# The matrix memories' query convolution moved from VectorE to TensorE as diagonal products

## What is computed

```python
def short_conv(a, w, b, n_ctx):
    a_ctx, a_lat = a[:, :n_ctx], a[:, n_ctx:]
    lat = lax.conv_general_dilated(a_lat.reshape(bsz, rows, GRID_W, ch), w[:, :, None, :], (1, 1), 'SAME', ...)
    ctx = lax.conv_general_dilated(a_ctx, w[CONV_K // 2][:, None, :], (1,), 'SAME', ...)
    return jnp.concatenate([ctx, lat.reshape(bsz, s_lat, ch)], axis=1) + b
...
qk = jax.nn.silu(short_conv(jnp.concatenate([ml_q, ml_k], axis=-1), conv_w, conv_b, n_ctx))
mq, mk = jnp.split(qk, 2, axis=-1)
```

## Time and profile before

| | |
|---|---|
| median of 3 runs | 3661.3 us (3655.49 to 3663.13) |
| the profiled execution | 3671.62 us, span 3668.6 us |
| busy over the span | PE 3333.2 us, DVE 1671.9 us, ACT 1162.1 us, POOL 975.9 us |
| busy from 2215 to 2269 us (54 us) | PE 15.41, DVE 50.84, ACT 21.05, POOL 2.35 us |

### The profile page before, as it was taken

The page is one execution under the profiler, slowest core; times in us unless marked ns, Lnnn a source line. Parts: engine busy times, 40 slices in busy tenths (PEclk is TensorE's granted clock), DMA queues, the critical chain, the costliest instruction groups (busy, mean ns, idle before and its releaser), DMA issues. The chain is left out here.

```text
span 3668.6 us, 42188 instructions
## 1 busy us (share of the span) xinstructions
PE 3333.2 (91%) x17058; PEld 2636.7 (72%) x17058; DVE 1671.9 (46%) x2620; ACT 1162.1 (32%) x1873; POOL 975.9 (27%) x418
## 2 busy tenths in 40 slices
PE   4999989989999799999998875989999888889998
PEld 3887767867888588888787662368887664568887
DVE  5995566554331323355500997532211585631211
ACT  2232364224443322122332213333223224533222
POOL 0001322433444122322332110024443220024443
PEclk7999999998999799999999997889999888889999
DMA  4232324441223122334321000012232110013332
GB/s 178 92 98 91 130 95 154 154 166 64 98 95 95 61 86 93 126 133 139 112 75 58 18 18 6 1 62 95 97 110 88 52 46 26 1 58 98 96 94 86
DMA packets 91197, 315.98 MB, mean 86 GB/s; under 512 B 10742, under 2 KB 12534, under 8 KB 90234
## 3 DMA queue, kind: packets, MB, share of 16 engines
q1 hardware_dynamic: 88060, 303.69, 25.6%
q10 hardware_dynamic: 2944, 9.60, 0.7%
HBM read 311.16 MB, written 2.10 MB: 85 GB/s over the span
## 5 line engine op out<-in xcount | busy, mean ns | idle before, releaser
L245 POOL TENSOR_TENSOR terms<-streams,terms 128x1024 fp32r<-128x1024 f32 (+2 forms) x414 | 975.6, 2357 | 2670.8 <-ACT terms L233 2670.8
L454 PE MATMUL bank<-terms,terms 128*128 128x512 f32 (+2 forms) x3936 | 1477.4, 375 | 49.1 <-DVE terms L721 17.7
L455 PE MATMUL bank<-terms,terms 128*128 128x512 f32 (+2 forms) x3936 | 1468.9, 373 | 0.0
L456 PE MATMUL bank<-terms,terms 128*128 128x512 f32 (+2 forms) x3936 | 1467.1, 373 | 0.0
L233 ACT ACTIVATE terms<-streams 128x1024 fp32r<-128x1024 f32 (+1 forms) x462 | 475.5, 1030 | 1802.1 <-PE bank L456 1624.8
L454 PEld LDWEIGHTS bank<-terms,terms 128*128 128x128 f32 x3936 | 749.3, 190 | 200.8 <-issue 52.1
L456 PEld LDWEIGHTS bank<-terms,terms 128*128 128x128 f32 x3936 | 749.1, 190 | 129.2
L455 PEld LDWEIGHTS bank<-terms,terms 128*128 128x128 f32 x3936 | 750.9, 191 | 123.5
L1642 DVE TENSOR_TENSOR stage<-stage,bank 128x256 f32<-128x256 f32 (+1 forms) x88 | 54.6, 621 | 596.6 <-ACT stage L1632 596.6
L1085 DVE SCALAR_TENSOR_TENSOR arena<-arena,vec 128x512 f32<-128x512 f32 x240 | 162.5, 746 | 0.2
L1625 DVE TENSOR_TENSOR terms<-stage,terms 128x512 fp32r<-128x512 f32 (+1 forms) x66 | 116.5, 1769 | 0.0
(11 more groups left out here) (334 smaller groups left out, 3133.1 us busy)
## 6 DMA issues: line engine op xcount, KB each, us to landing
streams<-in_ffn_w SPq DMA_DIRECT2D x104, 512.0 KB, 3.5
streams<-in_w_mod SPq DMA_DIRECT2D x72, 512.0 KB, 3.5
streams<-in_w_up SPq DMA_DIRECT2D x44, 512.0 KB, 3.5
streams<-in_w_gu SPq DMA_DIRECT2D x44, 512.0 KB, 3.5
streams<-in_w_ada SPq DMA_DIRECT2D x32, 512.0 KB, 3.5
streams<-in_w_down SPq DMA_DIRECT2D x32, 512.0 KB, 3.6
streams<-in_w_v SPq DMA_DIRECT2D x24, 512.0 KB, 3.8
streams<-in_ffn_w SPq DMA_DIRECT2D x24, 384.0 KB, 3.3
```

The lines of the kernel that those rows point to most:

```text
L245: gp.tensor_tensor(self.low(m), self.raw(n), self.high(m), ALU.subtract).then_inc(self.low_made.sem, 1)
L454: pe.matmul(out, high[:, at], x_high, start=kk == start, stop=False)
L455: pe.matmul(out, high[:, at], x_low, start=False, stop=False)
L456: mm = pe.matmul(out, low[:, at], x_high, start=False, stop=kk == kts - 1)
```

## The change

The two query tiles are no longer convolved by taps. ACT makes 18 weight matrices of 128x128 out of the identity, one for each tile and tap: the identity scaled by that tap's weight of each channel, a diagonal matrix. PE multiplies each with the shifted grid and accumulates the nine taps of a tile in one PSUM bank, in plain float32. ACT then adds the bias and takes the SiLU straight from the bank. DVE keeps the 24 taps of the keys, in the order 0 to 9, reciprocals, 9 to 15, scaling, 15 to 24.

```diff
+ML_DIAG = B2_QG + 1536
...
+    def diagonals(self, act):
+        for t in range(2):
+            for tap in range(9):
+                ins = act.activation(self.diagonal(t, tap), k.ident[:, :], ACT.Copy, scale=k.v("mconv_w", 9 * t + tap))
+            ins.then_inc(self.weights_made.sem, 1)
+
+    def smoothed(self, pe, t):
+        bank, uses = self.banks[t]
+        if uses:
+            pe.wait_ge(self.k.bank_free[bank].sem, uses)
+        pe.wait_ge(*self.weights_made(t + 1))
+        for tap in MIDDLE_FIRST:
+            r, c, rx, cx = self.ranges(tap)
+            mm = pe.matmul(grid(self.k.bank[bank][:, :])[:, r, c], self.diagonal(t, tap), grid(self.plain(t))[:, rx, cx],
+                           start=tap == 4, stop=tap == 8)
+        mm.then_inc(self.queries_in.sem, 1)
+
+    def queries_kept(self, act, t):
+        act.wait_ge(*self.queries_in(t + 1))
+        act.activation(self.queries[t], self.k.bank[bank][:, :], ACT.Silu, bias=self.k.v("mconv_b", t)
+                       ).then_inc(self.k.bank_free[bank].sem, 1)
...
-                            inputs.tapped: 42})
+                            inputs.tapped: 24, inputs.weights_made: 2, inputs.queries_in: 2})
+        inputs.banks = [k.take_bank() for _ in range(2)]
...
         self.heads.widened(pe)
+        for t in range(2):
+            self.inputs.smoothed(pe, t)
 
     def scalar(self, act):
         self.heads.squares(act)
+        act.wait_ge(*self.k.dve_done(HEADS2))
+        self.inputs.diagonals(act)
         self.heads.roots(act)
         self.gates.scalar(act)
         self.chain.softplus(act, self.gates)
-        act.wait_ge(*self.inputs.tapped(42))
         for t in range(2):
-            act.activation(self.inputs.queries[t], self.inputs.queries[t], ACT.Silu)
+            self.inputs.queries_kept(act, t)
+        act.wait_ge(*self.inputs.tapped(24))
+        for t in range(2):
             act.activation(self.inputs.keys[:, t, :], self.inputs.keys[:, t, :], ACT.Silu)
 
     def vector(self, dve):
...
-        self.inputs.taps(dve, 0, 12)
+        self.inputs.taps(dve, 0, 9)
         self.heads.inverses(dve)
-        self.inputs.taps(dve, 12, 24)
+        self.inputs.taps(dve, 9, 15)
         self.heads.scaling(dve)
-        self.inputs.taps(dve, 24, 42)
+        self.inputs.taps(dve, 15, 24)
```

More of the change, by code:

```diff
@@ L2050, in __init__ @@
         self.k = k
-        self.tapped = k.more[12]
+        self.tapped, self.weights_made, self.queries_in = k.more[12:15]
         k.bank_set, k.bank_turn = [3], 0
@@ L2104, in there, with ranges @@
         for t in range(2):
-            self.of_queries.evicted(eng, t)
             for c in range(2):
                 self.of_keys.evicted(eng, t, c)
+    def ranges(self, tap):
+        dy, dx = tap // 3 - 1, tap % 3 - 1
+        r, c = slice(max(0, -dy), 8 - max(0, dy)), slice(max(0, -dx), 64 - max(0, dx))
+        return r, c, slice(r.start + dy, r.stop + dy), slice(c.start + dx, c.stop + dx)
     def taps(self, eng, a, b):
@@ L2115, in tap @@
         k = self.k
-        t, j = divmod(n, 9) if n < 18 else (2 + (n - 18) // 12, (n - 18) % 12)
+        t, j = divmod(n, 12)
         if n:
@@ L2119, in tap @@
         if j < 9:
[L2120 to L2126, removed]
+            tap = MIDDLE_FIRST[j]
+            r, c, rx, cx = self.ranges(tap)
+            y, x = grid(self.keys[:, t, CTX:])[:, r, c], grid(self.plain(2 + t))[:, rx, cx]
+            w, first = k.v("mconv_w", 9 * (2 + t) + tap), j == 0
         else:
@@ L2130, in tap @@
             c = slice(max(0, -dx), CTX - max(0, dx))
-            y, x = self.keys[:, t - 2, c], self.context(t - 2)[:, c.start + dx:c.stop + dx]
-            w, first = k.v("mconv_w", 9 * t + 3 + tap), j == 9
+            y, x = self.keys[:, t, c], self.context(t)[:, c.start + dx:c.stop + dx]
+            w, first = k.v("mconv_w", 9 * (2 + t) + 3 + tap), j == 9
         if first:
-            ins = eng.tensor_scalar(y, x, w, k.v("mconv_b", t), ALU.mult, ALU.add)
+            ins = eng.tensor_scalar(y, x, w, k.v("mconv_b", 2 + t), ALU.mult, ALU.add)
         else:
@@ L2137, in tap, with diagonal @@
         ins.then_inc(self.tapped.sem, 1)
+    def diagonal(self, t, tap):
+        at = ML_DIAG + P * (9 * t + tap)
+        return self.k.arena[:, at:at + P]
+    def diagonals(self, act):
+        k = self.k
+        for t in range(2):
[8 more added lines that the diff above has]
+        for tap in MIDDLE_FIRST:
+            r, c, rx, cx = self.ranges(tap)
+            mm = pe.matmul(grid(self.k.bank[bank][:, :])[:, r, c], self.diagonal(t, tap), grid(self.plain(t))[:, rx, cx],
+                           start=tap == 4, stop=tap == 8)
+        mm.then_inc(self.queries_in.sem, 1)
+    def queries_kept(self, act, t):
+        bank, _ = self.banks[t]
+        act.wait_ge(*self.queries_in(t + 1))
+        act.activation(self.queries[t], self.k.bank[bank][:, :], ACT.Silu, bias=self.k.v("mconv_b", t)
+                       ).then_inc(self.k.bank_free[bank].sem, 1)
+MIDDLE_FIRST = (4, 0, 1, 2, 3, 5, 6, 7, 8)
 class MemoryStart(Pass):
```

## The result

In the first measurement the changed kernel takes 3642.56 us (median of 5, 3640.98 to 3644.66) against 3661.3 (5 runs, 3655.49 to 3666.45): the ratio is 0.9947, 95% interval 0.9936 to 0.9958, a gain of 19 us where 11.6 were forecast. Four more comparisons in three later sessions gave 8.0, 15.4, 9.9 and 12.8 us. (The ratio is not the quotient of the medians, which lie 9.3, 17.7, 9.7 and 10.2 us apart there; a gain worked out from a ratio is that share of the median of the kernel before.) The block itself is 10.8 to 10.9 us shorter in every trace.

What follows compares the result with a forecast made beforehand. DVE was taken to bound the query convolution's block; taking 11.6 us off it brings the profiled execution from 3671.6 to 3660.0, and 10.3 less for the median gives 3649.7 us. Its own range was 3645 to 3654, the whole range 3642 to 3657.

Steps and rivals of the forecast that it cites:

- The sum: Whole kernel: barrier 11.6 us earlier, profiled execution from 3671.6 to 3660.0, less 10.3 to the median: 3649.7 us.
- The third rival: Matrix memory: an earlier start moves the low-clock stretches; up to 3695 us, or 2 to 4 us gained; chance 0.04.
- The bound: Query convolution's block between two barriers: DVE, without a gap, sets its end; a microsecond off DVE is one off the kernel.
- The size of the block's gain: DVE from first tap to memset: two query tiles removed, 12.86 us, less waits; gain 11.6 us, within 11.0 and 12.8.
- GpSimd's wait: DVE's context taps: the third meets POOL's operation and waits 2.3 us, with bounds of 1.2 and 2.9.
- What ACT gets: ACT ahead of the roots: 18 scaled copies at 0.257 us each, 4.6 us, roots ready just when DVE needs them.
- the roots' row: ACT's four roots, 128 columns with one pointer operand, 0.257 us from start to start, taken as each diagonal's price.
- the page's price: Skill page's cost of an ACTIVATE: 0.29 us a diagonal, a stall of 0.7 us, a gain of about 11.1 us.
- What PE gets: PE behind the widening: 18 float32 matmuls, 8360 columns at 1.65 ns plus 0.14 us each, 16.4 us, hidden behind DVE.
- the first rival: PE's new matmuls run at 1.2 GHz: a gain of only 2.3 to 5.1 us, 3657.6 us; chance 0.15.

Runs made afterwards that it cites:

- 15 memsets: Changed kernel with 15 further idle memsets on VectorE ahead of the scans, meant to put the next block's start back: 3660.96 us.
- 12 of them: Changed kernel with 12 further idle memsets on VectorE ahead of the scans, for the old block length: 3663.97 us, ratio 1.0004 to the kernel before.
- changed_third: The changed kernel run anew without edit, as a control: 3644.77 us, ratio 0.9958 to the kernel before.
- roots_first: Changed kernel with the roots ahead of the diagonals on ScalarE: 3645.8 us, ratio 0.996 to the kernel before.
- no_queries: Changed kernel without the query convolution (no diagonals, new matmuls or bias; queries only pass the SiLU): 3650.43 us.
- under_pool: roots_first with 15 taps instead of 9 ahead of the reciprocals, so that these run beside GpSimd's operation: 3650.44 us, ratio 0.9967 to the kernel before.
- after_again: The changed kernel run anew without edit: 3649.29 us, ratio 0.9978 to the kernel before.

## Where the prediction failed, and what of it held

- **The sum is where the forecast failed.** It took the 11.6 us off one profiled execution, 3671.6 us, put the change of everything outside the block at nothing, and carried that execution's distance to a median of three over to the changed kernel. The parts outside are not fixed. Between the first two traces the spans differ by 29.4 us, of which the block gives 10.9; 5.5 lie ahead of it, 6.0 in the matrix memory and 7.0 behind, all in code that the change doesn't touch except for the bank numbers. In identical code, five traces of the changed kernel lie 5.1 us apart ahead of the block and 6.8 behind it (matrix memory and the rest); the first one's sum of all parts but the block is 3597.0 us, 8.5 under the lowest of the other four. In the matrix memory the difference is all clock, by the windows above. In the other two parts slower matmuls have a share: between the first two traces the same 10736 matmuls ahead of the block kept PE busy 2026.9 and 2020.3 us, the same 5862 behind the matrix memory 1179.0 and 1175.3.
- **The first 19 us are in good part luck.** The five executions of the changed kernel in the first measurement all lay at the low end (3641.0 to 3644.7) of what the 37 of all sessions spread over (3640.9 to 3657.7), its five of the kernel before at 3655.5 to 3666.5. The medians over all sessions are 3648.65 us (37 executions) and 3659.1 (98): 10.4 us apart, and the mean of the four later ratios, 0.9969, is 11.5 us. These agree with the block's 10.9 and lie near the forecast's 11.6, as far as sessions that scatter by 8 to 15 us can tell. The third rival had the mechanism, low stretches that move, but tied it to the earlier start and put a low stretch lost around 2340 at 2 to 4 us; the runs tie it to no edit at all, and it moved the matrix memory by 6.0.
- **The bound: right.** DVE set the block's end, and PE came back on its branch. The block grew by the 15 memsets' 13.68 us in full, and the kernel's median by 11.7 in the same session; with 12 of them the block grew by 10.9 and the median by 19.2 against changed_third, which shows how far medians scatter.
- **The size of the block's gain: 0.7 us too large.** Forecast 11.6 with bounds of 11.0 and 12.8, measured 10.8 to 10.9 in five traces, just outside. From the first tap to the memset it took 24.99 us for some 24.3 forecast: the reciprocals began 7.21 us behind the first tap instead of 6.43 (0.8 more), from their end to the second key tile it took 3.38 instead of 3.8 (0.4 less), and from there to the memset 11.10 instead of 10.8 (0.3 more).
- **GpSimd's wait: right in kind.** The forecast let the third context instruction meet GpSimd's operation and put the wait at 2.3 us. In the changed kernel it was the second, since the roots had come 0.81 us late; without that delay, in roots_first, it was the third. The one that met it took 2.48 us, 2.0 more than the other one's 0.5 (the two took 3.00 together).
- **What ACT gets: the size was off.** The term took 0.257 us a diagonal from the roots' row; the trace has 5.38 us for 18 of 0.387 us each, (5.38 - 0.39) / 17 = 0.294. That is the 0.29 worked out beside it from the Trainium skill, "ScalarE: Activation LUTs", what a table load costs: here the page's price held and the roots' row, of the same shape, did not carry over. The stall was 0.81 us, forecast none, 0.7 by the page. roots_first puts it at nought and gets 0.77 us back.
- **What PE gets: right in kind, 2.2 us too dear.** 14.19 us for 8360 columns are 1.70 ns each, with next to nothing per matmul on top. In the groups of two of the earlier trace rows the forecast read 0.14 us a matmul, 0.28 a group. Of that, 0.16 is the end of the group's last record, which lasts 0.59 us where records start 0.43 apart, and which a row of 36 records has only once; where the other 0.12 came from no run settles. The clock held at 1.00, so the first rival fell.
- **The 0.52 us behind the scaling** were in no term. They stand in the changed kernel, in no_queries and in roots_first, not in the kernel before nor in under_pool, which have 0.14 there. The row names DVE's own scaling as releaser; why the wait is longer no run settles.
- **What stays open.** Why five executions in a row came out at the low end. The values come in clusters (about 3641.5, 3649 and 3657 us among the changed), and which one is common differed by session. The chip alone isn't it: on one and the same chip, of after_again's 11 executions none lay under 3645 us, of changed_third's six three did; the chip of the first measurement is not on record. Whether the changed kernel meets the short matrix memory more often (3 of 5, against none of 3) is not decided by so few traces. That the shorter block, or the matmuls in it, sets this part alone is refuted: the same code had 118.7 and 124.7. And the two long ones already differ ahead of the block, where PE's last two products (L1911, L1912) took 0.64 us instead of 0.39.

## What to carry to other kernels

When a barrier ends a stretch on one engine whose timeline has no gap, its removed instructions count, less the waits that the new order brings (here 12.86 us of taps gave 10.9); then look at the second engine's end, since that is where the next microsecond stops counting (here ACT's softplus, all but reached by putting roots and reciprocals elsewhere). Before an engine is given work, ask what already stands behind that place in its order: 18 hidden copies cost 0.8 us only because the roots stood behind them. A forecast of a whole kernel's time also needs the scatter of what it leaves alone, from more than one trace. And where the granted clock changes between executions of the same code, judge an edit of a few tenths of a per cent by the length of its own stretch in two or three traces; a tight set of five executions (3641.0 to 3644.7) did not hold for the next session's eleven (3645.8 to 3656.3).

## What the runs showed of the hardware

- A TENSOR_SCALAR with one SBUF input, 512 float32 columns in 0.54 us, stood for GpSimd just as the taps with two inputs did (2.46 us), while four RECIPROCALs took 3.38 us beside the same operation and without it. The Trainium skill, "GPSIMD Engine Reference", specifications, names both kinds that contend, two inputs and two-port modes. The traces agree on two inputs; that the TENSOR_SCALAR ran in a two-port mode no row says, and its half nanosecond for a further column, against twice that for the taps, only fits it.
- Plain float32 matmuls of 441 to 512 columns, each with its own 128x128 weights, ran back to back at 1.70 ns a column at the 2.4 GHz level, with windows of a grid, gaps in every row of 64, among their inputs and outputs.
- The same 348 matmuls of the matrix memory cost 105.9, 108.9 or 112.0 us of busy PE, at mean granted clocks of 0.89, 0.86 and 0.84, in executions of identical code.
